# Two transformer-like blocks on one core: where the buffers of a kernel begin in SBUF

## What is computed

```python
def first_block(x, ...):
    for l in range(2):
        x = layer_norm(ALPHA * x + 0.5 * swiglu(x, ffn_w1[l, 0], ffn_w2[l, 0]), ...)
        mix = hybrid_mixer(x, w_in[l], ...)     # 1024 x 7168, gates, two 1024 x 1024, w_o
        x = layer_norm(ALPHA * x + mix, ...)
        x = layer_norm(ALPHA * x + 0.5 * swiglu(x, ffn_w1[l, 1], ffn_w2[l, 1]), ...)
    return x

def swiglu(x, w1, w2):                          # w1: 1024 x 5632, w2: 2816 x 1024
    g, u = jnp.split(x @ w1, 2, axis=-1)
    return (jax.nn.silu(g) * u) @ w2
```

## The kernel before, in words

| buffer | first byte | past a multiple of 64 | past a multiple of 256 |
|---|---|---|---|
| `ring`, `w_lo` | 16544 | 32 | 160 |
| `xrow` | 65696 | 32 | 160 |
| `w_hi` | 73888 | 32 | 160 |
| `z`, `bcast` | 98464, 106656 | 32 | 160 |
| `cr` (identity, cosines) | 116928 | 0 | 192 |
| `cv_pad` | 123936 | 32 | 32 |
| `x_lo`, `x_hi` | 128096, 136288 | 32 | 96 |
| `arena` | 144480 | 32 | 96 |

## Time and profile before

### The profile page before, as it was taken

One profiled execution on the slowest core, in us unless ns is written; L12 is line 12 of the kernel. 1 busy time (PEld: TensorE's weight loads), 2 busy tenths in 40 slices (PEclk: granted clock), 3 DMA queues, 4 the chain that ended last, 5 costly groups with the idle time before them and its releaser, 6 DMA issues.

```text
span 2166.9 us, 35416 instructions
## 1 busy us (share of the span) xinstructions
PE 2136.0 (99%) x14990; PEld 1938.4 (89%) x14990; DVE 1429.6 (66%) x2066; ACT 902.2 (42%) x1066; POOL 18.8 (1%) x36
## 2 busy tenths in 40 slices
PE   9999999999999999999999999999999989999998
PEld 8998999999989989999899768888788879999996
DVE  4556878675566548876756777887666447665665
ACT  4334366343343334384434352222344344443442
POOL 0000000000000000000000000000000000000000
PEclk9999999999999999999999999999999989999999
DMA  9654555666466555555575422222212232332331
GB/s 350 226 185 190 195 195 214 233 233 253 181 258 242 195 194 191 192 183 213 215 237 206 179 95 78 78 78 78 77 41 78 88 117 78 117 117 78 117 117 59
DMA packets 29005, 349.56 MB, mean 161 GB/s; under 512 B 2992, under 2 KB 5424, under 8 KB 8368
## 3 DMA queue, kind: packets, MB, share of 16 engines
q1 hardware_dynamic: 24672, 313.42, 39.3%
q0 software_dynamic: 4176, 33.89, 4.1%
HBM read 346.24 MB, written 1.05 MB: 160 GB/s over the span
## 4 chain that ended last, share of the span: by engine, by line
PE 94%; DVE 2%; ACT 2%; DVEq 1%; issue 0%; ACTq 0%
PE banks L921 13%; PE banks L780 12%; PE banks L775 12%; PE banks L776 12%; PE banks L1008 8%; PE banks L1086 6%; PE banks L1083 6%; PE banks L1082 6%; PE banks L792 2%; PE banks L1100 2%; PE banks L1096 2%; PE banks L1097 2%; PE banks L1277 2%; PE banks L1276 2%; PE banks L1278 2%; PE banks L878 1%
## 5 line engine op out<-in xcount | busy, mean ns | idle before, releaser
L2100 DVE TENSOR_TENSOR w_lo<-ring,w_hi 128x2048 fp32r<-128x2048 f32 x290 | 661.9, 2290 | 398.4 <-ACT w_hi L1514 394.3
L1514 ACT ACTIVATE w_hi<-ring 128x2048 fp32r<-128x2048 f32 x290 | 555.7, 1917 | 682.8 <-PE banks L780 453.9
L775 PE MATMUL banks<-x_hi,w_hi 128*128 128x256 f32 x2112 | 500.5, 279 | 0.5 <-ACT w_hi L1514 0.5
L776 PE MATMUL banks<-x_lo,w_hi 128*128 128x256 f32 x2112 | 499.4, 278 | 0.0
L775 PEld LDWEIGHTS banks<-x_hi,w_hi 128*128 128x128 f32 x2112 | 397.8, 188 | 1.5 <-issue 1.5
L776 PEld LDWEIGHTS banks<-x_lo,w_hi 128*128 128x128 f32 x2112 | 397.6, 188 | 0.0
L780 PE MATMUL banks<-x_hi,w_lo 128*128 128x256 f32 x2112 | 286.6, 278 | 1.0 <-DVE w_lo L2100 1.0
L780 PEld LDWEIGHTS banks<-x_hi,w_lo 128*128 128x128 f32 x2112 | 262.8, 188 | 1.4 <-DVE w_lo L2100 1.4
L1082 PE MATMUL banks<-x_hi,w_hi 128*128 128x512 f32 (+1 forms) x656 | 233.9, 369 | 0.0
L1083 PE MATMUL banks<-x_lo,w_hi 128*128 128x512 f32 (+1 forms) x656 | 227.2, 359 | 0.0
L1551 ACT ACTIVATE arena<-banks 128x512 f32<-128x512 f32 (+5 forms) x178 | 79.7, 471 | 286.3 <-PE banks L1086 165.0
(11 more groups left out here) (378 smaller groups left out, 2814.6 us busy)
## 6 DMA issues: line engine op xcount, KB each, us to landing
ring<-weights SPq DMA_DIRECT2D x147, 2048.0 KB, 7.7
arena<-mods POOLq DMA_DIRECT2D x11, 2048.0 KB, 11.2
bcast<-lnrows POOLq DMA_DIRECT2D x12, 512.0 KB, 5.1
ring<-weights SPq DMA_DIRECT2D x2, 1024.0 KB, 10.0
filt_sb<-filt POOLq DMA_DIRECT2D x2, 609.0 KB, 21.0
xrow<-x SPq DMA_DIRECT2D x1, 1024.0 KB, 5.2
arena<-hy_consts POOLq DMA_DIRECT2D x1, 1024.0 KB, 12.3
xrow<-ctx_rows POOLq DMA_DIRECT2D x1, 1024.0 KB, 5.7
```

Of the source, the lines that this page charges most:

```text
L775: nc.tensor.matmul(out, hi[:, k, t * P:(t + 1) * P], x_h[:, k, :], start=k == 0, stop=False)
L776: nc.tensor.matmul(out, hi[:, k, t * P:(t + 1) * P], x_l[:, k, :], start=False, stop=False)
L1514: nc.scalar.activation(hi, raw, ACT.Copy).then_inc(w_hi_done, 1)
L2100: v.tensor_tensor(lo, raw, hi.bitcast(F32), ALU.subtract).then_inc(w_lo_done, 1)
```

## The change

The first free byte is 16640, which is 65 times 256, and `at[0]` is rounded up to a multiple of 256 at two further places: ahead of `cv_pad` and ahead of `x_lo`.

```diff
+LINE = 256
...
-        at = [16544]
+        at = [16640]
...
         rs = place("rs", [P, 56])
+        at[0] = -(-at[0] // LINE) * LINE
         cv_at = at[0]
         cv_pad = place("cv_pad", [P, 2, 2 + SEQ])
         xr_pad = place("xr_pad", [P, 2, 3 + SEQ])
+        at[0] = -(-at[0] // LINE) * LINE
         xt_at = at[0]
         x_lo = place("x_lo", [P, KT, SEQ], F32R)
```

## The result

The changed kernel takes 2196.8 us, the median of its runs, beside 2164.4 us for the kernel before in the same comparison. The ratio is 1.0137, interval 1.0119 to 1.0155: it is 1.4% slower. The profiled execution took 2196.37 us with a span of 2194.5 us, 27.6 us more than before. In every run that lists both, the span is 1.8 to 1.9 us shorter than the time; so the profiled execution of the kernel before took some 2168.7 us, about 4 us above its median and not 2.1, and outside the range of its three runs. Most of the gap between the 27.6 us of the spans and the 32.4 of the medians is this. Of the four executions of the changed kernel one, at 7565 us, is counted as slow and left out; nothing on record says what held it up. All lines of after are numbered 3 higher from line 762 on: line 780 is 783, line 921 is 924, line 1086 is 1089.

The account below looks back on a forecast made before the run. TensorE's matmul spacing was taken to bound the kernel; savings at 256 and 512 columns, together 112.0 us, 94% counted, 105.3, took 2166.9 to 2061.6, less 2.1 to the median 2059.5, stated as 2060 us; range 2040 to 2168.

Parts of the forecast that it names:

- What bounds the kernel: Whole kernel: TensorE, busy 99% and 94% of the last chain, sets the end by how fast it gets through its list.
- The cover: Weight split on VectorE and ScalarE, and DMA: they still keep up with a faster TensorE, at no cost.
- What gets a worse place: Identity `cr`, now 32 bytes past a multiple of 64, streamed by some 400 float32 products and transposes: cost taken as nothing.
- What the excess looks like: float32r products: 113.3 ns is 272 cycles, 17 times 16, read as 17 pieces of 64 bytes touched instead of 16.
- The two terms of the sum: float32r products: 256 columns fall to 109 ns, saving 41.8 and 21.0 us; 512 to 216 ns, saving 32.4 and 16.8.
- the wide spacing: Slower spacing of 256-column products, 117.6 to 117.8 ns, taken for 4,860 of 9,744; in first feed-forward layers from the fifth block.
- the last step of the sum: Profiled execution to median of the runs: 2.1 us taken off 2061.6, giving 2059.5 us.
- the piece goes: Rival, float32r products: the piece goes, the second excess stays; 89.6 us less at the end, 2075 us, chance 0.13.
- only the second excess goes: Rival, float32r products: 16 cycles on 256 columns stay, the slow spacing goes; 34 us less, 2131 us, chance 0.12.
- Nothing happens: Rival: the excess belongs to float32r at full rate and 17 times 16 is chance; 2165 us, chance 0.18.
- Slower: Rival: buffers at the same place modulo 256 fix all float32r products at 117.8 and 233.3 ns; 27.5 us added, 2192 us, chance 0.15.
- The range: Kernel time: low end 2040 us if float32r even reached 106.7 and 213.3 ns, high end 2168 us for no change.

Follow-up runs that it names:

- misaligned_distance_0: The changed kernel with all its buffers 32 bytes further on, stationary and streamed operands still at distance 0 modulo 256: 2195.7 us, ratio 1.0135.
- aligned_distance_64: The changed kernel with its first buffer 64 bytes further on: weights 64 past a multiple of 256, activations at 0; 2164.8 us, ratio 0.9995.

## Why the prediction was wrong

**What bounds the kernel: right.** The chain is TensorE's for 94% after as before, and a change of some 31 us in its spacings came out as 28 to 32 at the end.

**The cover: right, but not put to the test.** The forecast let TensorE go faster; it went slower. The longest waits are the 4.3 and 2.3 us of the earlier trace rows. The weight split did not feel the new places either, 2289 ns on VectorE and 1915 on ScalarE beside 2290 and 1917:

```profile
L2103 DVE TENSOR_TENSOR w_lo<-ring,w_hi 128x2048 fp32r<-128x2048 f32 x290 | 662.1, 2289 | 427.2 <-ACT w_hi L1517 423.9
...
L1517 ACT ACTIVATE w_hi<-ring 128x2048 fp32r<-128x2048 f32 x290 | 555.1, 1915 | 715.2 <-PE banks L783 489.5
```

**What gets a worse place: right.** A transpose that streams the misplaced identity still takes 0.87/8 = 109 ns, so nothing was the proper price. The row that was used as a bound says less than was read from it: of the 1.5 ns by which products of 257 columns stood above those of 256, 0.8 ns is the one column more (two cycles, as 256 take 512), so that row is weak evidence of any loss by place.

**What the excess looks like: the step that failed.** "A slice of 1024 bytes that begins 32 bytes past a multiple of 64 touches 17 pieces of 64 bytes; one that begins on a multiple touches 16." All of the sum hung on that: 109 and 216 ns per product. In after every streamed slice begins on a multiple, and takes 120.0 ns. misaligned_distance_0 has 17 pieces in each and takes the same. The number 272 = 17 x 16 was only one sample; 120.0 ns are 288 cycles, 18 x 16, for slices of 16 pieces, and the excess at distance 0 is 13.3 ns with 256 columns and with 512, which pieces of 64 bytes can't give. In its place the runs show the distance of the two operands modulo 256, which the change took from 64 and 192 to 0. The prediction said that no row proved the reading, since every slice lay alike; but it gave readings that rest on it 0.67. The two terms of the sum, -62.8 us at 256 columns and -49.2 at 512, measured +45.3 and -14.0. Two smaller terms were off as well. The first feed-forward layers switch to the wide spacing at their eighth block (behind line 888, at 93 us), not the fifth, so that 44% of the products of 256 columns ran at it and not half, worth 2.5 us. And the last step of the sum, from span to median, took off 2.1 us where some 4 were due.

**The first two rivals** (the piece goes; only the second excess goes) rest on place in the same way and fell with it. Their argument was half right: place alone does not choose between the two spacings; what stands ahead of a stream does too. But at distance 0 there is only one.

**Nothing happens:** right in what it said of alignment. The rule cited there, the 16-byte lines of the Trainium skill's "SBUF — State Buffer", "Specifications (TRN2)", agrees with the trace in so far as a start at 32 past 64 costs nothing by itself (2195.7 beside 2196.8 us). But the change did something else beside aligning, it moved the two operands against each other, and so the 2165 us did not come; they did come in aligned_distance_64.

**Slower,** at 0.15 and 2192 us, named the mechanism: how weight loads and streams fall against each other, decided where both "begin at the same distance from a multiple of 256". Its total came within 5 us of the result, and that is partly luck. It priced all products at 117.8 and 233.3 ns; they take 120.0 and 227.2. One size was too small and the other had the wrong sign. What was held against it failed twice over. The `mt2_hi` group of line 1277 streams 512 columns, for which 0 is the best distance, and only 6 of its 16 tiles have it: the ones in `bcast` and `z`. The others have 192 (`arena`) and 128 (`cv_pad`), the products of `mt2_lo` between them 192, and the steps of the group are 230.1 ns in the mean and not the 226.7 of distance 0. And what was compared was the length of records (398 and 394 ns), when the prediction itself had said that only the distance between starts tells the spacing.

**The range,** 2040 to 2168, followed the chances, and they were put on one explanation of a number. The trace of before held what was needed for more doubt: two spacings with the same operands, and a change that makes all relative places equal, which no row of before had at 256 columns.

## What to carry to other kernels

Where one engine sets the end and one number per instruction is to change, a factorisation that fits that number is no evidence; look for a row in which only the suspected cause differs, and if there is none, give the other sign its share. Move both operands of a float32r product together or not at all: in a layout written by hand, look at stationary start less streamed start modulo 256 for each width of the streamed operand, here, with 128 stationary columns, 64 (or 192) for 256 columns and 0 for 512. A trick that improves a steady stream must be priced at its joins in the full kernel: the same transpose gained 10 us at 14 places and lost 10 at 74.

## What the runs showed of the hardware that was not expected

- The spacing of float32r products depends on the distance between its two operands modulo 256 bytes: 113.3 to 120.0 ns with 256 columns, 226.7 to 234.3 with 512, and the best distance for 512 columns is among the worst for 256. With 128, 192 and 320 columns distances 0, 64 and 192 made no difference. In float32 the transposes kept 109 ns when the change moved their operands by 64 bytes against each other; bf16 (109.2 ns) and float32 products (215.8 ns) were streamed alone at distance 0 only.
- At distance 0 a float32r product of 256 to 512 columns takes 13.3 to 16 ns more than its columns, whatever their number.
- At distances 64 and 192 a stream of 256 columns keeps 113.3 or 117.8 ns from its start on, by what came ahead of it and by the place: behind 96 columns of a transpose it is 113.3 with the operands at 96 and 160, and 117.8 with them at 160 and 224. At 96 and 160 all 26 short transposes, of 2 to 64 columns, gave 113.3.
- The number of stationary columns acts on the spacing of the stream: at distance 0 it is 120.0 ns with 128, 116.0 with 96 and 113.3 with 64 and 32; at distance 64 it is 119.1 with 64. Whether the reads of the two operands meet, or something else in it, is not shown.
- A transpose of 8 columns between float32r products costs 354 ns in the full kernel, of which its own step is 153; the rest is in the steps of its neighbours.
